# Recurrent mixer with paired level bursts and a second set of buffers, attention units one slot earlier: a four-layer hybrid trunk on one core

## The reference, cut to what matters

```python
def _hgrn2_mixer(h, w_in, norm_w, w_out, lb):      # 8 heads, key and value width 128
    proj = h @ w_in
    q = proj[..., :HGRN_FD].reshape(bsz, s, H, DK) * (DK ** -0.5)
    f = lb + (1.0 - lb) * jax.nn.sigmoid(proj[..., HGRN_FD:2 * HGRN_FD])
    ...
    def step(state, inp):
        qc, kc, vc, gc = inp
        cum = jnp.cumsum(gc, axis=1)
        decay = jnp.exp(jnp.where(causal, cum[:, :, None] - cum[:, None, :], -jnp.inf))
        attn = jnp.einsum('blhk,blshk,bshk->blsh', qc, decay, kc)
        o = jnp.einsum('blsh,bshv->blhv', attn, vc) + jnp.einsum('blhk,bhkv->blhv', qc * jnp.exp(cum), state)
    ...
def _swa_mixer(h, w_in, q_norm, k_norm, sinks, w_out, cos, sin):
    ...
    m = jnp.maximum(jnp.max(scores, axis=-1, keepdims=True), sink)
    p = jnp.exp(scores - m)
    denom = jnp.sum(p, axis=-1, keepdims=True) + jnp.exp(sink - m)
    o = jnp.einsum('bnhgqk,bnkhd->bnqhgd', p / denom, vw).reshape(bsz, s, nq)
```

## Time and profile before

| | |
|---|---|
| median of three runs | 1721.2 us (1720.79 to 1722.05) |
| the profiled execution's own time | 1720.66 us |
| its span in the profile | 1718.8 us |
| busy: PE / DVE / ACT / POOL | 98% / 67% / 63% / 72% |
| share of the chain that ended last | PE 81%, DVE 9%, ACT 6%, issue 3% |
| granted TensorE clock | full in every slice |
| attention mixer, from its first tile to its last unit | 897 to 1005 us of the span |
| HGRN2 mixer, from its first tile to its last tail | 1264 to 1455 us of the span |

### The profile page before, as it was taken

How to read it: one execution, slowest core, us unless ns; L and a number is a source line. 1 busy time by engine, 2 the same in 40 slices (tenths; PEclk the granted TensorE clock), 3 DMA queues, 4 the chain that set the end, 5 groups by cost and what they waited for, 6 DMA issues and landing times.

```text
span 1718.8 us, 27106 instructions
## 1 busy us (share of the span) xinstructions
PE 1691.6 (98%) x9708; PEld 1055.2 (61%) x9708; DVE 1143.1 (67%) x1966; ACT 1082.8 (63%) x1553; POOL 1232.4 (72%) x1777
## 2 busy tenths in 40 slices
PE   8999999999999999999999999999999999999999
PEld 4556666666666556666665666666656665666665
DVE  7986777228888855777328858775258886677720
ACT  8887666456767656666455776665555665866632
POOL 7866777877556657777877657778766553777786
PEclk9999999999999999999999999999999999999999
DMA  7334444556233225444444124444443332444443
GB/s 280 109 103 131 148 148 143 158 159 171 75 102 107 96 77 177 150 150 145 146 152 135 38 75 141 148 147 153 143 133 101 99 99 75 135 148 148 147 154 127
DMA packets 65614, 226.53 MB, mean 132 GB/s; under 512 B 8149, under 2 KB 9045, under 8 KB 65109
## 3 DMA queue, kind: packets, MB, share of 16 engines
q1 hardware_dynamic: 64236, 221.89, 40.3%
q10 hardware_dynamic: 1245, 2.92, 0.6%
HBM read 222.48 MB, written 2.10 MB: 131 GB/s over the span
## 4 chain that ended last, share of the span: by engine, by line
PE 81%; DVE 9%; ACT 6%; issue 3%; DMA 1%; POOL 0%; SPq 0%; DVEq 0%; ACTq 0%
PE psum L311 25%; PE psum L321 24%; PE psum L352 13%; PE psum L360 12%; DVE psum L1716 1%; ACT w_big L252 1%; PE psum L2391 1%; DVE arena L1761 1%; PE psum L1946 1%; PE psum L2427 1%; DMA w_panel<-in_ssd_in 1%; PE psum L1991 1%; DVE psum L1772 0%; ACT x_big L419 0%; DVE arena L1704 0%
## 5 line engine op out<-in xcount | busy, mean ns | idle before, releaser
L282 POOL TENSOR_TENSOR w_rest<-w_panel,w_big 128x256 bf16<-128x256 f32 x1660 | 1168.9, 741 | 414.5 <-ACT w_big L252 413.6
L311 PE MATMUL psum<-x_big,w_big 128*128 128x512 f32 x2248 | 590.0, 408 | 8.1 <-ACT x_big L419 6.4
L252 ACT ACTIVATE w_big<-w_panel 128x1024 fp32r<-128x1024 f32 (+1 forms) x414 | 416.9, 1032 | 181.2 <-PE psum L360 124.0
L321 PE MATMUL psum<-x_rest,w_rest 128*128 128x512 bf16 x2248 | 520.9, 380 | 0.2 <-DVE x_rest L533 0.2
L311 PEld LDWEIGHTS psum<-x_big,w_big 128*128 128x128 f32 x2248 | 418.0, 189 | 117.0 <-issue 14.2
L321 PEld LDWEIGHTS psum<-x_rest,w_rest 128*128 128x128 bf16 x2248 | 206.7, 98 | 264.3 <-issue 41.3
L781 DVE SCALAR_TENSOR_TENSOR psum<-ffn_raw,params,psum 128x512 f32<-128x512 f32 x352 | 264.5, 752 | 7.2 <-ACT psum L735 1.0
L773 DVE TENSOR_TENSOR ffn_raw<-psum,rstd 128x512 f32<-128x512 f32 x176 | 120.4, 686 | 140.8 <-PE psum L321 131.8
L735 ACT ACTIVATE psum<-ffn_raw,params 128x512 f32<-128x512 f32 x176 | 137.3, 782 | 100.2 <-DVE ffn_raw L773 95.9
L611 DVE SCALAR_TENSOR_TENSOR x_resid<-psum,x_resid 128x512 f32<-128x512 f32 x64 | 43.8, 689 | 219.8 <-PE psum L360 211.8
L352 PE MATMUL psum<-g_big,w_big 128*128 128x512 f32 x704 | 183.2, 411 | 0.0
(11 more groups left out here) (283 smaller groups left out, 1633.8 us busy)
## 6 DMA issues: line engine op xcount, KB each, us to landing
w_panel<-in_up SPq DMA_DIRECT2D x176, 512.0 KB, 3.5
w_panel<-in_dn SPq DMA_DIRECT2D x64, 448.0 KB, 3.2
w_panel<-in_ssd_in SPq DMA_DIRECT2D x41, 512.0 KB, 3.5
w_panel<-in_dn SPq DMA_DIRECT2D x32, 512.0 KB, 3.5
w_panel<-in_hgrn_in SPq DMA_DIRECT2D x32, 512.0 KB, 3.4
w_panel<-in_lru_in SPq DMA_DIRECT2D x18, 512.0 KB, 3.8
w_panel<-in_ssd_out SPq DMA_DIRECT2D x16, 512.0 KB, 3.4
w_panel<-in_swa_in SPq DMA_DIRECT2D x12, 512.0 KB, 3.5
```

What stands on the lines that cost most here:

```text
L252: act.activation(k.w1[:, slot, 0:words], k.w[:, slot, 0:words], ACT.Copy, scale=(SHIFT - 1) / SHIFT).then_inc(k.s("panel_big"), 1)
L282: rest = pool.tensor_tensor(k.w2[:, slot, a], k.w[:, slot, a], k.w1[:, slot, a].bitcast(F32), ALU.subtract)
L311: pe.matmul(out, k.w1[:, slot, q * m:(q + 1) * m], k.x1[:, q, :], start=q == 0, stop=False)
L321: mm = pe.matmul(out, k.w2[:, slot, q * m:(q + 1) * m], k.x2[:, q, :], start=False, stop=q == DT - 1)
```

## The change

HGRN2, TensorE: no burst at even levels; at odd levels 3, 5, 7 the bursts of two levels, one behind the other. For that, even updates write into a second pair of buffers (in `y_plain`), so that the old values stay readable, and the half of the queries and keys that an update doesn't touch is copied by ACT (`kept`, two copies of 128x256 at levels 2, 4 and 6). VectorE takes the masked results of both levels after the odd update. The last head's t0 stands three slots sooner and its other tail steps one slot sooner; one rest run of the output projection may start after half its panel (`HG_HALVED`); some roundings on ACT stand elsewhere.

Attention: units start in slot 8; in slots 8 to 10 the rotation of a tile stands after the unit's scores; the last tile's two halves stand in two slots; the copies of the sinks go from VectorE to ACT, and for units 0 to 2 the second PSUM copy too; an `early` step does the rest matmul first; GpSimd's scalings stand after other panels.

```diff
+HG_LAST = (-3, 0, 1, 2, 3, 4, 5, 6, 7)
+HG_HALVED = 4
...
+        spare = k.y[:, HG_H:HG_H + 4, :].rearrange("p (n h) s -> p n h s", n=2)
+        self.qps, self.kss = (self.qp, spare[:, 0]), (self.ks, spare[:, 1])
...
+def level_buffer(n):
+
+    return n // 2 % 2
...
     def level(h, n):                       # hgrn_tensor
...
-        elif n > 1:
+        elif n > 1 and n % 2:
             pe.wait_ge(k.s("hgrn_update"), 21 * h + 3 * (n - 1))
-            if h or n > 2:
-                pe.wait_ge(k.s("hgrn_attn"), HG_COPIES * h + (n - 1 if n > 2 else 0))
-            (wide if n > HG_NEAR else narrow)(h, n).then_inc(k.s("hgrn_level"), 1)
+            pe.wait_ge(k.s("hgrn_kept"), 3 * h + n // 2)
+            pe.wait_ge(k.s("hgrn_attn"), HG_COPIES * h + n - 1)
+            for m, buf in ((n - 1, 1 - level_buffer(n - 1)), (n, level_buffer(n - 1))):
+                (wide if m > HG_NEAR else narrow)(h, m, b.qps[buf][:, h % 2], b.kss[buf][:, h % 2]
+                                                  ).then_inc(k.s("hgrn_level"), 1)
...
+    def kept(h, n):                        # hgrn_scalar, called from level(h, n) for even n
+        B, to = LEVELS[n - 1], level_buffer(n)
+        act.wait_ge(k.s("hgrn_update"), 21 * h + 3 * (n - 1))
...
+        for bufs, half_ in ((b.qps, 0), (b.kss, 1)):
+            was, new = (in_halves(bufs[i][:, h % 2, :], B)[:, :, half_, :] for i in (1 - to, to))
+            copy = act.activation(new, was, ACT.Copy)
+        copy.then_inc(k.s("hgrn_kept"), 1)
...
+        if n % 2:                          # hgrn_vector
             dve.wait_ge(k.s("hgrn_level"), 7 * h + n)
             if n > 1:
+                dve.wait_ge(k.s("hgrn_kept"), 3 * h + n // 2)
+        update(h, n)
+        if n == 1:
+            attended(h, 1)
+        elif n % 2:
+            attended(h, n - 1)
+            attended(h, n)
...
-SWA_FIRST = 9
+SWA_FIRST = 8
+SWA_BOTH = 3
...
     def early(t, o):                       # swa_tensor
...
+        pe.matmul(out, k.w2[:, slot, at], k.y2[:, t, :], start=t == 0, stop=False)
+        pe.wait_ge(k.s("panel_big"), k.rounds(k.panel0["swa_out"] + panel))
+        pe.matmul(out, k.w1[:, slot, at], k.y1[:, t, :], start=False, stop=False)
```

More of the change, by code:

```diff
@@ L443, in residual_scalar @@
             round_ahead(act, k, job, last - 1 if n > 1 else last - 2)
+        if job == "hgrn_out" and o == 0:
+            round_ahead(act, k, job, last)
         act.wait_ge(k.s("banks_free"), k.evicted(job, o))
@@ L1944, in narrow, with wide @@
                 keys = slice(c * P + first, c * P + first + HG_BLOCK)
-                rhs = in_halves(b.qp[:, h % 2, keys], LEVELS[n - 1])[:, :, 1, :]
-                mm = pe.matmul(near[first:first + HG_BLOCK, c], b.ks[:, h % 2, keys], rhs, start=True, stop=True)
+                rhs = in_halves(qp[:, keys], LEVELS[n - 1])[:, :, 1, :]
+                mm = pe.matmul(near[first:first + HG_BLOCK, c], ks[:, keys], rhs, start=True, stop=True)
         return mm
-    def wide(h, n):
+    def wide(h, n, qp, ks):
         B = LEVELS[n - 1]
@@ L2148, in level @@
     def level(h, n):
[L2149 to L2157, removed]
+        if n == 0:
+            dve.wait_ge(k.s("hgrn_lb"), 14)
+            dve.wait_ge(k.s("hgrn_level"), 7 * h + 1)
+            attended(h, 0)
+            return
@@ new lines, in level, with update @@
+        update(h, n)
[4 more added lines that the diff above has]
+            attended(h, n)
+    def update(h, n):
+        B = LEVELS[n - 1]
+        pd = b.pd[n - 1].rearrange("p (n two) -> p n two", two=2)
+        first, second = pd[:, :, 0], pd[:, :, 1]
+        wide = [P, S // (2 * B), B]
+        to = level_buffer(n)
+        was = to if n % 2 else 1 - to
+        qp, new_qp = (in_halves(b.qps[i][:, h % 2, :], B)[:, :, 1, :] for i in (was, to))
+        ks, new_ks = (in_halves(b.kss[i][:, h % 2, :], B)[:, :, 0, :] for i in (was, to))
+        if n > 1:
+            dve.wait_ge(k.s("hgrn_update"), 21 * h + 3 * (n - 1))
+        else:
+            dve.wait_ge(k.s("hgrn_gates"), 3 * h + 3)
+        if h >= 2 and n == 2:
+            dve.wait_ge(k.s("hgrn_o"), h - 1)
+        dve.tensor_tensor(b.pd[n], first, second, ALU.mult).then_inc(k.s("hgrn_update"), 1)
+        dve.tensor_tensor(new_qp, qp, first.unsqueeze(2).to_broadcast(wide), ALU.mult
+                          ).then_inc(k.s("hgrn_update"), 1)
+        dve.tensor_tensor(new_ks, ks, second.unsqueeze(2).to_broadcast(wide), ALU.mult
+                          ).then_inc(k.s("hgrn_update"), 1)
@@ L2298, in swa_events @@
             ev.append(("stat", i, 0))
-        if 0 <= i < SWA_V:
+        if 0 <= i < SWA_V and v not in (0, 1, 2):
             ev.append(("rope", i, 0))
@@ L2594, in low @@
                                      ALU.mult, ALU.add).then_inc(k.s("swa_y_split"), 1)
-    do = {"tile": tile_, "normed": normed, "rope": rope, "score": score, "scale": last, "low": low,
-          "second": second}
+    do = {"tile": tile_, "last_tile": last_tile, "normed": normed, "rope": rope, "score": score, "scale": last,
+          "low": low, "second": second}
     for what, i, o in swa_events():
```

128 lines of the change are left out of this document (85 added, 43 removed).

## The result

The changed kernel took 1759.56 us (median of four, 1758.41 to 1763.16) against 1721.53 us of the kernel before (median of four). The ratio is 1.0225, 95% interval [1.0213, 1.0237]: 38.0 us slower, where the prediction said 36.6 slower, 1757.8 us. The profiled execution was the longest of the four, 1763.16 us with a span of 1761.3.

A forecast was written before the change was run, and what follows sets the result against it. TensorE, busy 98% of the span, bounds the kernel. HGRN2 mixer +41.6 us, its end -1.5, attention -3.5: +36.6 us on 1721.2, so 1757.8 us, range 1738 to 1775.

The forecast's parts named there:

- the copies are hidden: Rival, 4%: ACT finishes the copies before TensorE ends the half preceding the pair, leaving only gains; -7.8 us, 1713 us.
- Levels 2 and 3: HGRN2 pair waiting for ACT's copies: at least 1.3 us late, 2.8 by the stamps; 2.3 taken, eight heads, 18.4 us.
- the rival that I gave 15%: Stalls at their least, as VectorE and ACT catch up while TensorE stalls: +17 us, 1738 us; chance 15%.
- Levels 4 and 5: HGRN2 pair waiting for ACT's copies behind tanh, affine copies and rounding: 4.0 us late, seven times, 28 us.
- Heads 0 and 7 have fewer tails in the way: -2: HGRN2 mixer: first and last heads have fewer tail steps in the way, taking 2 us off the sum.
- a sign of being wrong: Wrong if the first pair waits longer, copies end before the preceding big half, or time grows in the FFN instead.
- the rival that I gave 7%: TensorE's clock falls to 1.2 GHz after each of fifteen stalls, one half at half speed: +30 more, 1788 us; 7%.
- What would show it: Head period about 28 us, TensorE's waits naming ACT's copies, hardly any at 6-7, clock 1.00, attention's reduction wait below 1 us.
- pairing: HGRN2: joining two levels' bursts saves breaks between long and short matmuls, 0.35 us a head, -2.8 us for eight.
- attention: Attention stage: -2 us from shorter waits for VectorE's reductions and -1.5 from early steps, together -3.5 us.
- the last head: End of HGRN2: earlier roundings and the halved wait save 1.5 us, between 0 and 3.
- the early step: Attention: with the rest matmul first, L352 and L360 may each take 0.23 us; 14 x 0.11, -1.5 us.

The follow-up runs named there:

- e1: Changed kernel with ACT's copies at levels 2, 4 and 6 put ahead of its half-tile work in the same slot: 1735.66 us, ratio to the kernel before 1.0082.
- e3: Changed kernel with two more ACT copies of the same size, into an unused buffer, before each pair of copies: 1773.67 us, ratio to the kernel before 1.0306.
- e5: As e1, and ACT makes level 6's copies before the previous head's step t4: 1716.87 us, ratio to the kernel before 0.9973.
- e6: As e5, and VectorE takes level 6's masked result before update 7 instead of behind it: 1714.94 us, ratio to the kernel before 0.9962.
- e9: Changed kernel with only level 2's ACT copies put ahead of the half-tile work: 1757.53 us, ratio to the kernel before 1.0212.

## Why the prediction was right

**The mechanism.** Copies on ACT behind the half tile's work, TensorE waiting for them at two of a head's three pairs: shown by the stamps of copies and pairs, by e1 (moving them takes those waits away), and by e3 (lengthening them lengthens thirteen of the fifteen waits by nearly as much). The rival "the copies are hidden" is out, and so is the one that blames VectorE's doubled work between pairs: with the copies moved in all three places (e5) it is in time.

**The sizes, where the sum was less good than its end.**

- *Levels 2 and 3*: 2.3 us in each of eight heads was forecast, 18.4. Measured 4.34 in the first, 1.50 to 1.53 in six, 0.85 in the last, 14.3. I split the lateness of VectorE between "its wait for level 2's burst, which goes" and "the rest"; all of it went. It evicted the output gate 0.22 us after TensorE was done, so the least chain (1.3) was the right one: at this pair the rival that I gave 15% came true.
- *Levels 4 and 5*: 4.0 in each of seven was forecast, 28. Measured 3.74, then 2.83 to 2.88, 20.9. The update took 0.78 us and not 1.3, and TensorE itself was later by 0.45 than counted, waiting for the subtraction before t4. The term was also too large as it was worked out: its own figures give 3.8 and not 4.0, and by the earlier trace rows t4 and the half behind it take 2.74 us (1331.27 to 1334.01) and not 2.5.
- *"Heads 0 and 7 have fewer tails in the way: -2"* was wrong in sign for head 0, which had the longest waits of all. For the first of them the trace says why. Half 7 ends there at 1278.8, and VectorE evicts it only at 1281.37, since it is at updates 1 and 2 from 1276.32 until then, with four passes over 128x256 of 0.94 to 0.96 us each beside GpSimd; the copies end at 1285.24 and the pair starts at 1285.34. In this head the first wait, 4.34 us, was also longer than the second, 3.74, which the prediction had named as a sign of being wrong; in the other six it was shorter.
- *Two waits had no term.* The level 0 burst waits for the mask of level 6, which VectorE now takes behind update 7 (5.2 us in all), and t4 waits for the subtraction (2.7). The second was in the prediction's own figures, the subtraction over at 4.7 and TensorE at t4 from 4.2 on, and I never asked who waits there; for the first it had no figure.
- *The clock* fell in some heads, the rival that I gave 7%. It didn't decide: 1 us or less in the median, some 4 in the longest execution, not 30. I had priced half a tile at half speed after *every* wait; in the profiled execution five of the fifteen were followed by a lower clock, the two of the first head and three of 2.83 to 2.88 us.
- *What would show it*: the head period came out at 27.4 to 29.1 us (about 28 forecast; 25.8 for the last), the waits for the reductions in attention at 0.7 us (below 1), and hardly any wait at levels 6-7 (0.46 us, once), as said. That the clock would stay at 1.00 was wrong, and TensorE's waits didn't name ACT: the view put them down to "issue".
- *The gains*: pairing 3.2 us (2.8 forecast; a head of e6 takes 21.8 us from t4 to t4 where one of the kernel before took 22.16), attention 2.2 (3.5), the last head 1.2 (1.5, within the noise). In attention the early step did what was forecast where a single step stands between two bursts, in eight slots. There L2510 at 973.80 is followed by the transposes at 974.26, 0.46 us where L352 and L360 took 0.57, but not where two stand together, which cost the same before.

Added up: waits 35.2 + 5.2 + 2.7 (from the profiled execution), less 3.2 + 2.2 + 1.2 of gains, is +36.5, and 1 or so for the clock; measured +38.0. The forecast's +36.6 agrees because 11 us too much at the pairs, 9 after the -2, stood against 8 us of waits not thought of, 1.2 us of gains that didn't come and the clock. The direction and the place were well founded; that the number fits to 2 us was luck.

The step that carried the prediction was the comparison in the earlier trace rows: the end of a rounding on ACT at 1337.85 and the start of a burst at 1334.01, which had nothing to do with each other until the change.

## What to carry to other kernels

When an engine with idle time gets a new job for which the busiest engine waits, its share of busy time says nothing; ask what stands ahead of the job in its order, and when that can end. The same copies were behind most of 38 us where they stood, and ahead of that work, in e5, they left 1 us of waits at all the pairs together. And when waits stand in a chain, price them together: taking the first away can move the rest into a worse neighbour (e9 won 2 us, e1 24, e5 43), so a partial repair that brings little is no evidence against its cause.

## What the runs showed of the hardware

Waits of one length didn't have one effect on the clock. In the changed kernel's profile the waits before levels 4-5 were 2.83 to 2.88 us in six heads running; after three of them the granted clock was lower (0.56 in the 6 us from 1324 on, the pair having started at 1323.38), after three it stayed at full (here from 1410 on, the pair having started at 1409.30):

```profile
1324.00:1330.00 6.00, 5.67 (x47) 3.52 (x41) 4.14 (x10) 3.68 (x6) 2.40 (x4) 0.56 0.28 90
...
1410.00:1416.00 6.00, 5.79 (x56) 3.59 (x56) 5.75 (x13) 3.50 (x6) 3.60 (x6) 1.00 0.30 93
```

From the second head on, a head with the lower clock took 28.2 to 29.1 us from pair to pair, one without 27.4. The clock falls before the wait is over: it was 0.75 in the us from 1322 on and 0.50 from 1323 to 1329. After the six waits of 1.50 to 1.53 us it never fell; after e1's six of 2.24 to 2.27 us it fell three times, and after e9's seven of 3.57 to 4.51 us every time. A value of 0.56 is one near half, the lower of the two levels (1.2 and 2.4 GHz), for most of the stretch. And a wait for another engine's copies can stand in the list of waits as "issue"; the copies' own stamps, 0.1 us before the burst, name it.
